# Log-decay sums formed once in the projections, reloaded in the recurrence, and a reordered 64-row level in a hybrid three-branch token mixer

## What is computed

```
def gated_delta_chunked(q, k, v, log_a, beta):
    g = jnp.cumsum(log_a, axis=-1)
    g_last = g[..., -1]
    diff = g[..., :, None] - g[..., None, :]
    ...
    decay_strict = masked_exp(diff, strict)
    decay_causal = masked_exp(diff, causal)
    m = jnp.einsum('bhntk,bhnsk->bhnts', k, kb) * decay_strict
    rhs = jnp.concatenate([v, k * jnp.exp(g)[..., None]], axis=-1)
    sol = lax.linalg.triangular_solve(eye + m, rhs, left_side=True, lower=True, unit_diagonal=True)
    a_qk = jnp.einsum('bhntk,bhnsk->bhnts', q, kb) * decay_causal
    q_inter = q * jnp.exp(g)[..., None]
    k_state = kb * jnp.exp(g_last[..., None] - g)[..., None]
    ...
        state = jnp.exp(gl)[..., None, None] * state + jnp.einsum('bhlk,bhlv->bhkv', ks, e)
```

## Time and profile before

| | |
|---|---|
| median of 3 runs | 2814.27 us (2812.1 to 2814.34) |
| profiled execution | 2807.13 us, span on the core 2805.4 us |
| mean granted TensorE clock | 0.987 of full speed |
| busy | PE 2720.1 (97%), PEld 2273.4 (81%), DVE 1833.2 (65%), ACT 1237.3 (44%), POOL 1468.8 (52%) |
| projections | to 1627 us |
| recurrence, prologue and window 0 | 1627 to about 1700 us |
| recurrence, windows 1 to 14 | 1703 to 2228 us, 37.6 to 37.8 us each |
| window 15 | to about 2261 us |
| merge | to the end |

### The profile page before, as it was taken

How to read it: one execution, slowest core, us unless ns; L and a number is a source line. 1 busy time by engine, 2 the same in 40 slices (tenths; PEclk the granted TensorE clock), 3 DMA queues, 4 the chain that set the end, 5 groups by cost and what they waited for, 6 DMA issues and landing times. The chain is left out here.

```text
span 2805.4 us, 39318 instructions
## 1 busy us (share of the span) xinstructions
PE 2720.1 (97%) x14107; PEld 2273.4 (81%) x14107; DVE 1833.2 (65%) x2906; ACT 1237.3 (44%) x2150; POOL 1468.8 (52%) x1132
## 2 busy tenths in 40 slices
PE   7999999999997999999999979999999999999999
PEld 5788888888886888888888858888888877888887
DVE  7777777772337788787832248888888864445353
ACT  7443444444444434443444435655566543222221
POOL 0555555555545555555545466677766534453540
PEclk9999999999999999999999979999999999999999
DMA  6333333334363333333344366555566567555562
GB/s 190 98 113 93 103 109 103 97 105 110 101 173 110 116 98 104 92 113 105 91 113 115 92 158 155 133 136 135 145 156 157 134 181 238 165 184 169 176 178 74
DMA packets 537000, 366.03 MB, mean 130 GB/s; under 512 B 65526, under 2 KB 469096, under 8 KB 536808
## 3 DMA queue, kind: packets, MB, share of 16 engines
q1 hardware_dynamic: 536808, 363.52, 45.7%
HBM read 251.27 MB, written 112.20 MB: 130 GB/s over the span
## 5 line engine op out<-in xcount | busy, mean ns | idle before, releaser
L767 POOL TENSOR_TENSOR w_low<-w_raw,w_high 128x512 fp32r<-128x512 f32 x479 | 684.8, 1435 | 636.3 <-ACT w_high L846 636.2
L800 PE MATMUL p_x<-h_high,w_high 128*128 128x512 f32 x1280 | 500.7, 391 | 13.2 <-ACT u L975 6.5
L800 PE MATMUL p_x<-h_high,w_low 128*128 128x512 f32 x1280 | 499.9, 391 | 0.0
L800 PE MATMUL p_x<-h_low,w_high 128*128 128x512 f32 x1280 | 499.7, 390 | 0.0
L846 ACT ACTIVATE w_high<-w_raw 128x512 fp32r<-128x512 f32 x479 | 296.3, 626 | 247.8 <-PE p_z L800 141.3
L800 PEld LDWEIGHTS p_x<-h_high,w_high 128*128 128x128 f32 x1280 | 241.2, 188 | 66.6 <-ACT u L975 7.3
L800 PEld LDWEIGHTS p_x<-h_low,w_high 128*128 128x128 f32 x1280 | 241.4, 189 | 50.3
L800 PEld LDWEIGHTS p_x<-h_high,w_low 128*128 128x128 f32 x1280 | 241.3, 189 | 50.0
L800 PE MATMUL p_z<-h_high,w_high 128*128 128x512 f32 x640 | 249.0, 389 | 0.0
L800 PE MATMUL p_z<-h_high,w_low 128*128 128x512 f32 x640 | 249.0, 389 | 0.0
L800 PE MATMUL p_z<-h_low,w_high 128*128 128x512 f32 x640 | 249.0, 389 | 0.0
(11 more groups left out here) (303 smaller groups left out, 5983.2 us busy)
## 6 DMA issues: line engine op xcount, KB each, us to landing
w_raw<-in_w_in_dram SPq DMA_DIRECT2D x160, 512.0 KB, 5.2
branch_scratch<-ring SPq DMA_DIRECT2D x176, 256.0 KB, 5.2
gate_scratch<-ring SPq DMA_DIRECT2D x96, 256.0 KB, 6.0
ring<-gate_scratch SPq DMA_DIRECT2D x96, 256.0 KB, 4.0
hin<-branch_scratch SPq DMA_DIRECT2D x16, 1280.0 KB, 11.6
zin<-branch_scratch SPq DMA_DIRECT2D x16, 1024.0 KB, 7.1
m_wo_raw_lead<-in_w_out_c_dram SPq DMA_DIRECT2D x43, 256.0 KB, 3.0
xin<-in_x_dram SPq DMA_DIRECT2D x16, 512.0 KB, 4.2
```

The costliest lines, as they stand in the source:

```text
L767: nc.gpsimd.tensor_tensor(wl(j), place(p, j), wh(j).bitcast(F32), ALU.subtract).then_inc(low, 1)
L800: x = nc.tensor.matmul(to[:], w(j)[:, k, :], h[:, j, k, :], start=(opens and k == 0 and a == 0), stop=(k == HK - 1 and a == 2), skip_group ...
```

## The change

The sums of the log decays no longer come from the recurrence. In the projections TensorE forms them for all windows at once (at `p == 8`: four small matmuls over all 16 windows and 8 heads: sum up to t, sum after t, whole window, and sum up to t less the sum up to the window's middle), ScalarE copies them (`p == 9`), TensorE turns two of them (`p == 10`), ScalarE copies these (`p == 11`), and SyncE stores both to HBM (`p == 12`). POOL makes the causal mask at `p == 3` already, VectorE derives two masks at `p == 6`. In the recurrence SyncE loads the sums once (`col`) and, for each window, the two rows spread over all 128 partitions: `load_centred` and `load_start`, 512 KB each. POOL's `exponents(v)` subtracts and clips at zero instead of `log_decays`; ScalarE takes its exponentials from SBUF; the eight 128x512 matmuls of a window and their places in TensorE's order go. The factor from the window's start is one ScalarE instruction of 1024 columns where it was two of 512.

Apart from that `level_64` does its transposes first, and two of its four transposes go (the block they filled is not read); `level_w` of the last level then waits for one transpose of its half only, and `level_z` for the copies.

```
-                pe.wait_ge(zeroed, 2)
-                columns()
                 norms(0)
-                decays_between(0)
-                decays_from_start(0)
                 products_kq(0)
...
-                    if 0 < w < win - 1:
-                        decays_between(v)
                     level_z(w, 4)
                     if 0 < w < win - 1:
                         products_kq(v)
                     if w > 0:
                         scores(w, 0)
-                    if 0 < w < win - 1:
-                        decays_from_start(v)
                     level_w(w, 5)
...
                     for g in range(2):
                         wait(dve, w, "m_z", 2 + g + 1)
-                        for at in (0, 64):
+                        nc.vector.transpose(TT[32:64, 4 * g:4 * g + 4, 0:32], G[g][0:32, :, 0:32]).then_inc(sems["t_half"], 1)
+                    for g in range(2):
+                        for at in (64, 0):
                             left, right, packed = slice(at, at + 32), slice(at + 32, at + 64), slice(at // 2, at // 2 + 32)
                             nc.vector.tensor_copy(R[left, 4 * g:4 * g + 4, right], G[g][packed, :, packed]).then_inc(sems["r_turned"], 1)
-                            nc.vector.transpose(TT[right, 4 * g:4 * g + 4, left], G[g][packed, :, packed]).then_inc(sems["t_half"], 1)
...
-                def log_decays(v):
-                    wait(pool, v - 1, "m_ga", 2)
-                    for i in range(2):
-                        tt(la_t[:, i, :, :], free_ap(masks["causal"][:], 0, [[0, V], [1, P]]), spread(la_parts[:, i, v, :].bitcast(F32), P),
-                           ALU.mult).then_inc(sems["la_ready"], 1)
+                def exponents(v):
+
+                    pool.wait_ge(centred_in, 16 * v + 16)
+                    if v == 0:
+                        pool.wait_ge(col_in, 16)
+                    wait(pool, v - 1, "aq_ready", 2)
+                    tt(dec[:], rows_centred[:], spread(col[:, 3, v, :], P), ALU.subtract).then_inc(sems["diff_ready"], 1)
+                    wait(pool, v, "diff_ready", 1)
+                    nc.gpsimd.tensor_scalar(dec[:], dec[:], 0.0, None, ALU.min).then_inc(sems["diff_ready"], 1)
...
+                def decay_sums_of():
+
+                    pe.wait_ge(causal_cut, 1)
+                    pe.wait_ge(sum_masks, 2)
+                    for i, which in enumerate((causal[:], after, keep["ones"][:], centred)):
+                        x = nc.tensor.matmul(sums_bank[:, i, :], which, ab[:, :, 0:dm.vh], start=True, stop=True)
+                    x.then_inc(decay_sums, 1)
+
+                def decay_rows_of():
+                    pe.wait_ge(sums_kept, 1)
+                    for i, at in enumerate((0, 3)):
+                        x = nc.tensor.transpose(rows_bank[:, i, :], kept_sums[:, at, :], keep["ident"][:])
+                    x.then_inc(decay_rows, 1)
...
                 def decays_between(v):
-                    if v > 0:
-                        wait(act, v - 1, "ak_ready", 2)
-                        wait(act, v - 1, "aq_ready", 2)
+                    wait(act, v, "diff_ready", 2)
                     for g in range(2):
-                        wait(act, v, "m_gb", g + 1)
-                        fn(four(dec, g), M[g][:], ACT.Exp).then_inc(sems["dec_ready"], 1)
+                        fn(four(dec, g), four(dec, g), ACT.Exp).then_inc(sems["dec_ready"], 1)
```

More of the change, by code:

```diff
@@ L784, in _ @@
                 pool.wait_ge(low, form_no[N - 1, P3])
[L785 removed]
+                fill_masks(pool, front["masks"], masks_set, masks_cut)
             @block.tensor
@@ L1395, in _, with load_centred, load_start @@
                 of_c = tiles["q"]
+                rows = front["decay_rows"]
+                def load_centred(v):
+                    wait(sp, v - 1, "diff_ready", 1)
+                    sp.dma_start(rows_centred[:].rearrange("p h n -> p (h n)"), bass.AP(rows.tensor, (win + v) * V * P, [[0, P], [1, V * P]])
+                                 ).then_inc(centred_in, 16)
+                def load_start(v):
+                    wait(sp, v - 1, "eg_ready", 1)
+                    sp.dma_start(rows_start[:].rearrange("p h n -> p (h n)"), bass.AP(rows.tensor, v * V * P, [[0, P], [1, V * P]])
+                                 ).then_inc(start_in, 16)
                 def load_k(w):
@@ L1448, in lead_in @@
                         sp.dma_start(lead["wraw"][:, k, :, :], io[name][0][:, 0:P].rearrange("(k p) c -> p k c", p=P)).then_inc(lead_done, 16)
+                sp.dma_start(col[:].rearrange("p i w c -> p (i w c)"), front["decay_sums"]).then_inc(col_in, 16)
+                load_centred(0)
+                load_start(0)
                 load(0)
-                sp.wait_ge(zeroed, 3)
+                sp.wait_ge(zeroed, 1)
                 for d in inv_dram:
@@ L1454, in _ @@
                 load_k(1)
+                load_centred(1)
+                load_start(1)
                 blocks_out(0)
@@ L1571, in _ @@
                 mm, turn, ident = nc.tensor.matmul, nc.tensor.transpose, keep["ident"][:]
-                def columns():
-                    for i, which in enumerate((masks["causal"][:], later_r[:].bitcast(F32), keep["ones"][:])):
-                        x = mm(G[0][:, i, :], which, ab[:, :, 0:V], start=True, stop=True)
-                    x.then_inc(m_col, 1)
                 def norms(v):
@@ L1890, in level_exp @@
                     elif l == 2:
-                        wait(act, w + 1, "eg_ready", 2) if more else wait(act, w, "kt_ready", 1)
+                        wait(act, w, "kt_ready", 1)
                     elif l == 3:
@@ L1894, in level_exp @@
                     elif l == 4:
-                        wait(act, w + 1, "eg_ready", 1) if more else wait(act, w, "hv_ready", 1)
+                        wait(act, w, "hv_ready", 1)
                     else:
```

123 lines of the change are left out of this document (65 added, 58 removed).

## The result

The changed kernel takes 2840.03 us (median of 4 runs, 2828.27 to 2841.6) against 2813.26 for the kernel before (4 runs): a ratio of 1.0088, 95% interval 1.0075 to 1.0102. It is slower by 0.9%, outside the forecast range. Ratios throughout are of each kernel to the kernel before as timed in the same session, and they leave out one run of 3408.49 us at a clock of 0.753, one of the ten of e1_level64, which its median still counts.

What follows compares the result with a forecast made beforehand. VectorE was taken to bound each window's first half, TensorE its tail, with X's landing a third limit. Terms +1.3 + 7.0 - 1.0 - 5.9 = +1.4 gave 2808.5 us profiled, 2815.7 as median; range 2798 to 2830.

Steps and rivals of the forecast that it cites:

- The reading of the bound: In a window, VectorE runs without a gap up to level_128; TensorE is the slow one from products_e to the norms.
- The step that failed: Windows 1 to 14: removing the decay matmuls, 2.02 us a window, only leaves TensorE idle, so 0 us.
- rival 4: TensorE's short idle pieces halve its clock from level_w to products_e in 15 windows: +61, 2877 us; chance 0.05.
- The step on X: The 64-row level saves VectorE 0.66 us in nine windows; seven others wait longer for X and gain 0: -5.9 us.
- The prologue: Five loads, 2.36 MB, ahead of the first X cost +7.0 us; window 1's four matmuls leaving the path give -1.0.
- The clock's shift: Window 0 runs partly at half clock and stays so: 0, with 2 us either way.
- The -1.0 for the matmuls that went: Prologue: window 1's four decay matmuls leave the path between scores(0, 0) and products_kq(1): -1.0 us, range 0 to -2.0.
- The projections: Before the recurrence, TensorE's four small matmuls and two transposes add +1.3 us, range 1.0 to 2.5.
- GpSimd: Each window, subtraction and clip take 1.9 to 4.8 us, taken as 3.0, against 3.8 before; hidden, so 0.
- 1: X lands in time everywhere, so all 16 windows gain 0.66 us: -3.4, 2810.9 us; chance 0.14.
- 2: TensorE is the bound after all, so 2.02 + 0.59 us come through in 14 windows: -30.4, 2783.9 us; chance 0.09.
- Rival 3: The prologue's four broadcast loads take 7.5 us each, one after the other: sum +24.4, 2838.7 us; chance 0.11.

Runs made afterwards that it cites:

- e1_level64: The kernel before with only the new 64-row level and its changed waits; the decay matmuls stay: 2807.48 us, ratio 0.9984.
- e10: The kernel before with only the stores of y moved behind the load of X: 2810.0 us, ratio 0.9999.
- e12: The changed kernel with the old 64-row level and the stores of y behind the load of X: 2850.79 us, ratio 1.0133.
- e6: The changed kernel with the two stores of y placed behind the load of X: 2814.83 us, ratio 1.0011.
- e11: The changed kernel with the stores of y behind the load of X and idle matmuls at both places of the decay matmuls: 2805.47 us, ratio 0.9971.
- e5: The changed kernel with a window's two spread rows loaded behind T and R instead of directly behind X: 2868.15 us, ratio 1.0196.
- e8: The changed kernel with the two spread rows of window 1 loaded behind the first X in the prologue: 2834.9 us.
- e13: The changed kernel with y stored behind X, both idle matmuls, and window 1's spread rows loaded behind the first X: 2806.76 us.
- e15: The changed kernel with y stored behind X, both idle matmuls, and window 1's spread rows and the zero writes behind the first X: 2808.28 us.
- e9: The kernel before with the new 64-row level and the stores of y behind the load of X; decay matmuls stay: 2797.74 us, ratio 0.9939.
- e14: The kernel before with the new 64-row level, y stored behind X, and the prologue's two zero writes behind the first X: 2796.4 us.

## Why the prediction was wrong

**The reading of the bound was right.** VectorE paces the first half, TensorE the second, and the decay matmuls were hidden work for the most part: their 28 us did not come through. A part did: 0.58 us a window where the clock holds (e10 against e12), 7.5 us in 13 windows, which I had put at 0. VectorE comes to `X` that much sooner (21.15 and 20.58). Window against window the difference arises between `an_keys` and `level_pred(w, 2)`: small waits for TensorE of 0.05 and 0.06 us, which the waits' view doesn't list, and operations that take longer, `kql` by `hx` most, 1.11 us against 0.91; why it is longer stays open.

**The step that failed: "By the reading above they turn into idle time of TensorE: 0."** They turned into idle time, and it was not free. Behind it the granted clock went to half for about 7 us per window, in the half that TensorE sets, +2.06 us on B, 26.9 in 13 windows. This is rival 4, to which I gave 0.05. My evidence against it was window 15 at clock 1.00; but that window loads no `X`, and its rows show one gap ahead of `products_e`, of 0.59 us, where e6 has 1.06 us a window and the changed kernel up to 2.6. The price, +61, took the half-clock ratio over a whole stretch in 15 windows; a fall lasts only about 7 us, so it came to less than half of that. What the Trainium skill reports ("TensorE: Matmul & The Clock Gate", section "A second HAM failure mode: psum-queue depth-cycling"), a kernel whose TensorE idles briefly and often between groups of matmuls and swings between the two levels, was the better guide, and the traces agree: 12 falls in 13 windows, 0 in e11 where the gaps are filled.

**The step on X was right in kind, wrong in size.** I counted 0.66 us sooner at `X`, a gain in nine windows and none in seven, -5.9. VectorE came 1.31 us sooner, 0.67 by the 64-row level (e1) and the rest with the decays, so all 13 windows waited for the landing: A fell by 0.07 us. And the landing itself came about 0.5 us later, by the loads behind it (e5); I had put these at 0, since they are "ahead of `XI`", and not asked what they share with `X`. Together with the first cause this is one chain: a wait for `X` on VectorE becomes a gap on TensorE at `scores(w, 4)`, and the gap brings the clock down (e1). A new wait that costs nothing in A can be paid for in B.

**The prologue** was forecast at +7.0 and -1.0 and came to +9.4. The bytes were priced well: 2.36 MB moved the first `X` by 8.3 us, close to the upper bound of 8.1; I took a value between two rates where the lower one was that of this very place. But that this delay is the prologue's cost is not shown, since an earlier `X` gave nothing back (e8, e13, e15). The clock's shift, which I put at 0 with 2 us either way, was from 0.76 to 0.66 here. The -1.0 for the matmuls that went did not show.

**The projections**: the start of the recurrence did not move (1627.13 and 1627.10; other profiles lie from 1625.3 to 1630.6). The eight records of the four sums lie between 224.7 and 225.4 us, under 1 us together, below what this start can tell.

**GpSimd**: the clip takes more than my upper bound of 2.4 us, the subtraction the 1.9 foreseen:

```profile
L1554 POOL TENSOR_SCALAR dec<-dec 128x1024 f32<-128x1024 f32 x16 | 44.6, 2786 | 1.4
L1552 POOL TENSOR_TENSOR dec<-rows_centred,col 128x1024 f32<-128x1024 f32 x16 | 30.4, 1900 | 16.0 <-DMA rows_centred<-decay_rows_scratch 16.0
```

It was hidden in the windows of the changed kernel, as forecast, and is not once `X` is early: `products_o` waits 0.50 us in e6 at the end of that chain. The Trainium skill's rule ("GPSIMD Engine Reference", section "Engine selection"), that one-input operations run at about line rate on this engine and two-input ones some 2x slower than on VectorE, pointed the wrong way: from it I estimated about 1 us for the clip, and the one-input operation takes 2.79 us, the two-input one 1.90.

**The rivals**: 1 and 2 are out (the wait for `X` grew, the time did not fall). Rival 3, slow broadcast loads, is out: a spread row of 512 KB lands 4.5 or 5.0 us after its issue in the median, with two under way at a time, and the four ahead of the first `X`, with `col` 2.36 MB, moved it by 8.3 us, not by 30.

**Still open**: e10, with decay matmuls and no wait for `X`, shows four falls in its profile, and nine of e1's ten runs lie between 2794.89 and 2818 us. The kernel before may stand near the edge too: a gap of 0.59 us at `level_w` is the only one over 0.15 us ahead of `products_e` in the windows of e10 with a fall. Which gap of which length brings the clock down was not measured, only that fewer and shorter gaps went with fewer falls. The counts of falls are of one execution each.

**A version that beats both** is e9: the new 64-row level, the decay matmuls kept, the stores of y behind the load of `X`: 0.9939 (0.9919 to 0.9959), 2797.74 us. e14 is the same within its interval (0.9935). Of the change's decays nothing is in it. Against e11, which holds the clock too but forms its decays the new way, e9 has its windows start 10 us sooner (71.00 and 81.19 us to the norms of window 1), more than the 7.7 us between their medians.

## What to carry to other kernels

Before you take hidden work away from TensorE, ask what is left there: if it is a row of short waits just ahead of a stretch that TensorE sets, price that stretch at half clock for part of its length too. Ask also which engine comes next: here GpSimd's longer chain took back what the matmuls gave as soon as `X` was early. A transfer whose landing has 0.6 us to spare is a wall for every gain in front of it; here moving the stores of y behind it came first, and only then did the shorter engine pay. And check a stretch that the edit doesn't touch: here B, not A, carried the loss.

## What the runs showed that was not expected

- Matmuls that compute nothing made the changed kernel faster with `X` early: 2814.83 to 2805.47 us with two per window (e6 and e11). Without that the medians are 2840.03 and 2829.06, with ratios that overlap.
- In the changed kernel a fall of the clock lasts about 7 us in nine windows (from 1928 to about 1935 in the one shown), though TensorE is busy in it but for 0.56 us near its start; a fall costs 1.5 to 2.7 us of B.
- Two 512 KB loads issued 0.65 us behind a 64 KB load delay its landing from 2.8 to 3.3 us in the mean, though they stand behind it in the same queue.
- GpSimd's clip of 128x1024 takes 2.79 us, its subtraction of two such operands 1.90, and the longer chain ends in a wait of TensorE for ScalarE's `e`, two engines further on.
